# Attention slots of the two layers: running maps ahead of an older head's normalisation on TensorE, ScalarE and VectorE

## The reference

```python
def mixing_layer(h, ...):
    u = h @ w_in
    y_a = a_b * causal_depthwise_conv(a_c * a_x, short_conv_w)          # 3 taps
    q, k = rope(q), rope(k)                                             # 4 heads, 2 maps of 64 each
    lam = exp(sum(lam_q1*lam_k1)) - exp(sum(lam_q2*lam_k2)) + lam_init
    a = softmax(q0 k0, causal) - lam * softmax(q1 k1, causal)           # per head
    o = rmsnorm(a @ v, diff_subln_g) * (1 - lam_init)                   # per head, over 128
    y_c = silu(layernorm(causal_depthwise_conv(glu(c), conf_dw_w)))     # 31 taps
    return concatenate([y_a, o, y_c]) @ w_out

for l in range(2):
    x = x + mixing_layer(rmsnorm(x), ...)
    x = x + swiglu(rmsnorm(x))
```

## Time and profile before

| | |
|---|---|
| median of 3 runs | 1903.23 us (1902.68 to 1904.91) |
| the profiled execution | 1903.58 us, of which the span is 1901.8 us |
| PE matmuls busy in the span | 1871.3 us (98%) |
| POOL, DVE, ACT busy | 1107.8, 848.2, 728.7 us |
| layer 1, slots s = 22 to 43 | from 804 to 910 us of the span |
| layer 2, the same slots | from 1380 to 1486 us |

### The profile page before, as it was taken

One profiled execution on the slowest core, in us unless ns is written; L12 is line 12 of the kernel. 1 busy time (PEld: TensorE's weight loads), 2 busy tenths in 40 slices (PEclk: granted clock), 3 DMA queues, 4 the chain that ended last, 5 costly groups with the idle time before them and its releaser, 6 DMA issues.

```text
span 1901.8 us, 28880 instructions
## 1 busy us (share of the span) xinstructions
PE 1871.3 (98%) x8664; PEld 1504.2 (79%) x8664; DVE 848.2 (45%) x1309; ACT 728.7 (38%) x1159; POOL 1107.8 (58%) x1310
## 2 busy tenths in 40 slices
PE   7999999999999999999999999999999999999998
PEld 6876668888888888767888888888867888888886
DVE  7677643455555121786533323112686443332212
ACT  5245553433322222476433323223466432332222
POOL 5442226567676665765565666666776566566554
PEclk9999999999999999999999999999999999999999
DMA  7111112223222232312222222232321222222232
GB/s 251 67 56 45 45 56 100 95 85 108 90 98 99 100 110 100 118 57 71 88 90 100 93 96 98 100 109 100 120 64 62 82 96 100 99 89 99 102 108 77
DMA packets 51732, 176.94 MB, mean 93 GB/s; under 512 B 6480, under 2 KB 7632, under 8 KB 51408
## 3 DMA queue, kind: packets, MB, share of 16 engines
q1 hardware_dynamic: 51664, 176.04, 26.8%
HBM read 168.71 MB, written 2.10 MB: 90 GB/s over the span
## 4 chain that ended last, share of the span: by engine, by line
PE 88%; DVE 6%; ACT 2%; DVEq 1%; issue 1%; DMA 1%; SPq 0%; ACTq 0%
PE bank L540 22%; PE bank L520 22%; PE bank L521 22%; PE bank L577 3%; PE bank L578 3%; PE bank L584 3%; PE bank L781 1%; PE bank L827 1%; ACT lp L1312 1%; DVE lp L1419 1%; PE bank L813 1%; PE bank L560 1%; PE bank L554 1%; PE bank L555 1%; DVE bank L1419 1%; PE bank L629 1%
## 5 line engine op out<-in xcount | busy, mean ns | idle before, releaser
L465 POOL TENSOR_TENSOR wl<-raw,wh (+1 forms) x1244 | 1020.6, 852 | 734.2 <-ACT wh L1024 733.1
L1024 ACT ACTIVATE wh<-raw 128x1024 fp32r (+1 forms) x311 | 329.7, 1060 | 829.7 <-PE bank L540 690.0
L520 PE MATMUL bank<-xh,wh 128*128 128x512 f32 x1336 | 524.5, 393 | 0.4 <-ACT lv L1024 0.4
L521 PE MATMUL bank<-xl,wh 128*128 128x512 f32 x1336 | 521.3, 390 | 0.0
L540 PE MATMUL bank<-xh,wl 128*128 128x512 f32 x1336 | 340.1, 394 | 0.0
L520 PEld LDWEIGHTS bank<-xh,wh 128*128 128x128 f32 x1336 | 251.7, 188 | 58.5 <-issue 4.8
L540 PEld LDWEIGHTS bank<-xh,wl 128*128 128x128 f32 x1336 | 249.1, 188 | 60.6 <-issue 10.4
L521 PEld LDWEIGHTS bank<-xl,wh 128*128 128x128 f32 x1336 | 251.6, 188 | 51.8
L520 PE MATMUL bank<-hh,wh 128*128 128x512 f32 x528 | 205.4, 389 | 0.0
L521 PE MATMUL bank<-hl,wh 128*128 128x512 f32 x528 | 205.4, 389 | 0.0
L1463 DVE TENSOR_TENSOR ybuf<-bank,rstd 128x512 f32<-128x512 f32 x95 | 65.3, 689 | 239.8 <-PE bank L540 237.9
(11 more groups left out here) (302 smaller groups left out, 2188.9 us busy)
## 6 DMA issues: line engine op xcount, KB each, us to landing
raw<-in_weights SPq DMA_DIRECT2D x311, 512.0 KB, 3.5
turned<-ybuf SPq DMA_DIRECT2D x64, 64.0 KB, 2.0
xs<-in_x SPq DMA_DIRECT2D x4, 512.0 KB, 6.8
out_t<-xs SPq DMA_DIRECT2D x8, 256.0 KB, 2.0
w1k<-in_w SPq DMA_DIRECT2D x1, 1024.0 KB, 9.5
w1v<-in_w SPq DMA_DIRECT2D x1, 1024.0 KB, 10.8
shifted<-kvraw SPq DMA_DIRECT2D x8, 124.0 KB, 2.4
posi<-in_positions SPq DMA_DIRECT2D x2, 256.0 KB, 8.6
```

The lines of the kernel that those rows point to most:

```text
L465: x_ = pool.tensor_tensor(wl[:, :, :].rearrange("p s n -> p (s n)")[:, two], raw[:, cols((v % 4) * (CB * P) + h * part, part)], wh[:, :, : ...
L520: mm(b[:, :], w, kh(k), start=first and k == 0, stop=False)
L521: mm(b[:, :], w, kl(k), start=False, stop=False)
L1024: return act.activation(o, i, ACT.Copy, scale=scale)
```

## The change

`head_step` is divided. `map_step` holds what serves a head's maps, `norm_step` its normalisation, and in each slot an engine runs all `map_step`s ahead of the `norm_step`s. On PE the slot with step 2 puts the score ahead of the older head's values and its own transpose. On DVE the reciprocal moves from step 7 to step 8, inside `map_step` and behind `combine`, and all of this stands ahead of `peak`; `rot_end` moves from the head of its slot to behind the peaks. On ACT `y_head` goes behind the products, and the copy of BC moves from the head of slot 29 to the end of slot 28; DVE's taps are given to earlier chunks for it. `eps_rows` becomes a pair. A rest of `ya0` moves from slot 38 to 39, and one drain is added. In the diff the first part is PE's, the second ACT's (whose `map_step` holds `put` and `exps`, and `norm_step` the copy, the square and the root), the third DVE's.

```diff
-                def head_step(h, step):
+                def map_step(h, step):
+                    if step == 2 and h:
+                        score_l(h, 2)
+                        values_l(h - 1)
+                        turn_l(h, 0)
+                        return
                     if 2 <= step < 6:
                         turn_l(h, step - 2)
                     if step < 4:
                         score_l(h, step)
-                    if step == 6:
+                    if step == 6 and h == 3:
                         values_l(h)
+                def norm_step(h, step):
                     if step == 7:
                         pe.wait_ge(sq_ready, Count(8 + h).loop(l, 4).value())
-                        mm(STAT[:, 0:NT], ident, eps_rows, start=True, stop=True)
+                        mm(STAT[:, 0:NT], ident, eps_rows[h % 2], start=True, stop=True)
...
                     for h, step in steps:
-                        head_step(h, step)
+                        map_step(h, step)
+                    for h, step in steps:
+                        norm_step(h, step)
...
-                        if s == 29:
+                        for h, step in steps:
+                            map_step(h, step)
+                        for h, step in steps:
+                            norm_step(h, step)
+                        made_now = POOL_TAPS.get(n + 1, 0) - (n == 5)
+                        products(made_now // 2 + (made_now % 2 if half == 0 else 0))
+                        if s == 28:
                             act.wait_ge(R["conv_done"], L1.value())
                             copy(conv[:, 0, :], BC[:, :]).then_inc(R["conv_out"], 1)
+                        for h, step in steps:
+                            if step == 9:
+                                act.wait_ge(R["head_normed"], Count(h + 1).loop(l, 4).value())
+                                y_head(f"head{h}", lo_[:, h % 2, :])
...
-                def head_step(h, step):
+                def map_step(h, step):
+                    if step == 8:
+                        recips(U0 + NORM_OF_HEAD[h], NT)
                     if 1 <= step < 5:
                         combine(h, step - 1)
-                    if step < 4:
-                        peak(h, step)
-                    if step == 7:
-                        recips(U0 + NORM_OF_HEAD[h], NT)
+
+                def norm_step(h, step):
                     if step == 9:
...
-                BANK_TAPS = {5: (1, 1), 6: (1, 1), 7: (1, 1), 8: (2, 2), 9: (2, 2), 10: (2, 2), 11: (1, 1), 12: (2, 2),
-                             13: (2, 2), 14: (3, 0)}
+                BANK_TAPS = {5: (1, 1), 6: (1, 2), 7: (1, 2), 8: (2, 2), 9: (2, 2), 10: (3, 2), 11: (1, 1), 12: (2, 2),
+                             13: (2, 2)}
...
+                        for h, step in reversed(steps):
+                            map_step(h, step)
+                        for h, step in steps:
+                            if step < 4:
+                                peak(h, step)
+                        for h, step in steps:
+                            norm_step(h, step)
                         if half == 1 and qk_tile(n - 1) is not None:
                             rot_end(qk_tile(n - 1))
-                        for h, step in steps:
-                            head_step(h, step)
                         taps(BANK_TAPS.get(n, (0, 0))[half])
```

More of the change, by code:

```diff
@@ L237, in build @@
         sub_gain = small[:, 128:129]
-        eps_rows = small[:, 132:136]
+        eps_rows = [small[:, 132:136], small[:, 164:168]]
         zero4 = small[:, 160:164]
@@ L1315, in exps @@
                         act.wait_ge(R["exp_ready"], (SS + (8 * h + 8)).value())
-                        act.activation(eps_rows, rows2[:, r0:r0 + 2 * NT:2], ACT.Square, scale=float(np.sqrt(P * EPS)))
+                        act.activation(eps_rows[h % 2], rows2[:, r0:r0 + 2 * NT:2], ACT.Square, scale=float(np.sqrt(P * EPS)))
                 def put(h, i):
@@ L1337, in head_step @@
                         root(U0 + NORM_OF_HEAD[h], NT, scale=1.0 / P, bias=zero)
-                    if step == 9:
-                        act.wait_ge(R["head_normed"], Count(h + 1).loop(l, 4).value())
-                        y_head(f"head{h}", lo_[:, h % 2, :])
                 for n in range(4):
@@ L1374, in _ @@
                             y_head("ya0", ya[:, 0, :])
-                        for h, step in steps:
-                            head_step(h, step)
-                        made_now = POOL_TAPS.get(n + 1, 0) - (n == 5)
-                        products(made_now // 2 + (made_now % 2 if half == 0 else 0))
                         if s == 22:
@@ L1954, in _ @@
                     for half, (s, steps) in enumerate(layer_slots(n)):
+                        for h, step in reversed(steps):
[5 more added lines that the diff above has]
+                            norm_step(h, step)
                         if half == 1 and qk_tile(n - 1) is not None:
                             rot_end(qk_tile(n - 1))
-                        if s == 38:
-                            dve.wait_ge(R["tap_added"], Count(TAPS - 1).loop(l, TAPS - 1).value())
+                        taps(BANK_TAPS.get(n, (0, 0))[half])
+                        if s == 39:
                             y_rest("ya0", ya[:, 0, :])
-                        for h, step in steps:
-                            head_step(h, step)
-                        taps(BANK_TAPS.get(n, (0, 0))[half])
                         if s == 38:
@@ L1994, in _ @@
                         if what == 0:
+                            dve.drain()
                             take(tl, nl_, tmp3[:, 0:S])
```

## The result

The change takes 1926.56 us (median of 4 runs, 1922.14 to 1926.73), the kernel before 1903.60 us beside it (4 runs). The ratio is 1.0113, 95% interval 1.0100 to 1.0126: 23.0 us slower. The direction was forecast, the size was not: 1917 was said, and the measured time lies 2.6 us above the range of 1907 to 1924.

A forecast was written before the change was run, and what follows sets the result against it. PE was taken as the bound, matmuls filling 98% of the span, so only its gaps and lower clock count. Added waits 18.6 less 8.0, plus 3.3 for the clock, on 1903.58 gave 1917 us; range 1907 to 1924.

The forecast's parts named there:

- The credit: PE's attention waits removed because scores get operands and banks sooner, except those kept in slots 27 and 37: 8.0 us.
- slot 29: PE asks for score(1,3) at 833.9, before exps(1,2) ends at 834.4: an added wait of 0.6 us per layer.
- Spread(0): Slot 30: PE's spread waits for head 0's reciprocals, standing behind a DVE product that waits for ACT: 3.3 us per layer.
- the one with a drain of 1.38 us: Alternative price of ACT's table load, about 2.66 us: slot 30's wait 1.4 us longer, the sum 2.8 us larger.
- Spread(3): Slot 42: PE's spread waits for head 3's reciprocals, now behind n = 20's take and short convolution: 3.2 us per layer.
- Spread(1): Slot 34: DVE needs 5.8 us to the reciprocals, PE 4.9 to its spread: wait put at 1.0 us.
- spread(2): Slot 38: DVE needs 5.5 us to the reciprocals, PE 4.25 to its spread: wait put at 1.2 us.
- The taps: Extra DVE taps in chunks 6, 7 and 10, covered by idle time before slot 22; otherwise 0.8 us each, once.
- The waits together: Both layers' added waits of 18.6 us less the 8.0 us of waits removed: +10.6 us.
- forecast signs: Trace signs: L928 waits shrink from nine to some four; L637 waits for reciprocals eight times, some 17 us.
- The clock: Low-clock stretches after slots 30 and 42, sometimes 37 and 38, 1.7 us each: 6.6 against 3.4 now, taken as +3.3 us.
- the clock answers every long wait, and runs low in the layer norm's part too: Rival: six to eight stretches of 1.7 us in place of two, slot 30's chain stretched: 1922 to 1926 us, chance 0.17.

The follow-up runs named there:

- e10_ones30: The change, with sixteen useless one-column matmul calls (32 matmuls in the trace) per layer behind spread(0) in slot 30; 1939.1 us.
- e5_both: The change, with DVE's reciprocals back at step 7 and the extra taps of chunks 6 and 7 moved to slots 21 and 22; 1898.1 us.
- e1_recips7: The change, with each head's reciprocals on DVE back at step 7, ahead of the slot's product; 1900.5 us.
- e4_taps: The change, with DVE's taps of chunks 6 and 7 as before and the two left over given to chunks 10 and 11; 1919.98 us.
- e11_filler37: e5_both with five unread 512-column matmuls ahead of score(3,3) in slot 37; 1895.68 us.

## Why the prediction was right in direction and wrong in size

- **The credit.** It kept 0.8 us in slot 27, 1.8 in slot 37, and 1.2 in slot 29. Measured are 0.38 in each slot 27, 1.19 and 0.58 in slot 37, and nothing in slot 29. The last was wrong in its reason: it set PE's time by the old trace. PE comes to score(1,3) at 835.41 and not at 833.9, 1.5 us later, of which it was 1.3 late already in slot 27 (825.03 against 823.69). DVE and ACT were only 0.8 us late: exps(1,2) ends at 835.35, before at 834.51. So it had just ended. 1.2 us too much.
- **Spread(0): 3.3 us.** Measured 3.35 and 3.36, by the chain as it was put: root behind the table load, `ybuf`, product, combine, reciprocals. All absolute times were 0.8 us later on both sides. The load took 1.28 us, with the root 0.02 us behind it (839.88 to 841.18), so the sum by rows held, and not the one with a drain of 1.38 us.
- **Spread(3): 3.2 us.** Measured 3.16 and 3.14.
- **Spread(1) 1.0 and spread(2) 1.2 us.** Measured 0.23 and 1.74, 0.75 and 0.74. The two of spread(1) differ by 1.51 us: combine(2,3) took 0.75 us in layer 1 and 1.82 in layer 2 (see below), and the first product of `rot_end` 0.94 and 1.38. All spreads: 17.4 said, 16.4 measured.
- **The taps, "costed at nothing" with a price of 0.8 us each if the cover failed.** It failed: L608 has 2.2 us more. Ahead of the instruction for which PE waits DVE had only 0.58 us of idle time in the kernel before (at 783.03), for two taps of 0.8 us.
- **The waits together.** +10.6 us said, which is 12.0 of idle time less 1.4 for starts, and 11.7 of idle time measured. Right, with errors that cancelled: slot 29 and the spreads were 2.2 us too much, the taps 2.2 too little. Of the forecast signs, four waits at L928 and some 17 us at L637 came true.
- **The clock: the step that failed.** It said that 1.93 stretches of 1.7 us in each layer follow, 6.6 us and +3.3 over before. (If each of the two smaller waits is taken once in three, as the words have it, the bracket is 1.6 + 0.67 and the term 7.7 us, which changes little.) There were 30.7 us at 1.2 GHz, nine times 3.4 us, and PE's busy time grew by 10.8, where the forecast holds 3.3 less the 1.4 for starts, 1.9. That is 8.9 us, the whole distance between the span's 22.5 us and the 13.9 said, but for 0.3 the other way in idle time. That all four waits over 3 us are followed by a lower clock was nearly in the sum (four in five), and two of the smaller ones did so too, those of 1.74 and 0.74 us in slots 34 and 38 of layer 2. What it missed is how long it stays low: behind slot 42 it was 6.8 and 10.2 us in place of the 3.4 of which 1.7 was priced. The text named the layer norm's sixteen one-column matmuls there, and took them as a reason for one stretch, where with them it was two and three. e10_ones30 shows that such matmuls, 32 of them, prolong it in slot 30, and the eight cases of slot 42 against the ten of slot 30 that sixteen go with two or three. The rival "the clock answers every long wait, and runs low in the layer norm's part too", 1922 to 1926 at 0.17, was nearest to what happened; its upper end still lies 0.6 us under the median.

So the loss is one line of DVE's order, paid with 16.4 us of waits and another 8 to 10 through the clock that these waits bring down. The rest gains a little: with the line and the taps put right the change is worth 5.7 us (1903.85 beside it, to 1898.1), and a filler makes it 7.9.

What stays open is why of waits alike in length one is followed by a low clock and the other is not. It is so for 0.74 us in slot 38 of the change's two layers, for 1.30 us in slot 37 of e5_both's (3.4 us low and none) and e1_recips7's (3.4 and 6.8), and even for 3.35 us: in e4_taps slot 30 of layer 1 keeps its clock of 1.00. So the number of stretches is partly luck in each run. The four runs of the change span 4.6 us, and their mean clocks say that this is the clock: 0.990 three times, and 0.992 in the fastest; 0.002 of 1922 us is 3.8 us, as near to the 4.6 as three decimals can tell.

## What to carry to other kernels

When one engine's order is turned round, list for every semaphore who asks and who answers, and look at the new last instruction in front of the answer: here a reciprocal of 0.16 us went behind a short convolution of 4.7 us. Price a wait of PE with what follows it: the wait of slot 42, followed by small matmuls, cost 6.3 us of idle time here and up to 8.5 us through the clock. Where such a wait can't be removed, unread matmuls of about its length gave back 8 us in one slot of each layer and 14 in all, and 2.4 in a kernel that was already tight.

## What the runs showed of the hardware

- The clock can stay at 1.2 GHz while PE shows no idle time: 10.2 and 13.7 us in e10_ones30, with 32 one-column matmuls behind the wait with which it began. The Trainium skill, "TensorE: Matmul & The Clock Gate", "HAM oscillation — how this bites in real kernels", tells of a clock that falls in kernels that wait for DMA; here no DMA was waited for, and the waits ended with a reciprocal of 0.16 us on another engine.
- A wait of 1.30 us was enough in layer 1 of e5_both, and filling it took the stretch away (e11_filler37); the same wait in layer 2 was not followed by one.
- The same DVE instruction, combine's join of two maps, took 0.75 us at 865.94 and 1.82 us at 1450.50. Beside the second one, POOL ran an addition of 1.26 us from the same moment, beside the first one only from 866.39 on. DVE and then POOL, layer 2:

```profile
1450.50 1.82 DVE L1434 SCALAR_TENSOR_TENSOR lp<-lp,small 128x512 f32<-128x512 f32 x1
1452.24 0.17 DVE L1455 RECIPROCAL small<-small 128x4 f32<-128x4 f32 x1
```

```profile
1450.51 1.26 POOL L485 TENSOR_TENSOR conv<-conv,tprod 128x512 f32<-128x512 f32 x1 [2.62 <-ACT tprod L1034]
```

The extra 1.07 us is part of PE's wait of 1.74 us in slot 34. The Trainium skill, "GPSIMD Engine Reference", "Specifications", says that POOL shares its interfaces to SBUF with VectorE, with contention when a DVE instruction has two inputs there; the rows agree, and no run here took POOL's addition away to test it.
